# Gates' unit of the mLSTM: remainder and rounded weights in one stationary tile, and the norm's sums one unit later

## The chip, the cores and the metric

The kernel runs on one core of a Trainium2 chip. The metric is the device time of one execution in microseconds (us); 1,000 nanoseconds (ns) are 1 us.

## The reference, cut to what matters

The program is a transformer block followed by an mLSTM layer and an RG-LRU layer over 512 tokens of width 1024, all in fp32. The change lies at the start of the mLSTM layer:

```
u = rmsnorm(x, ln_g)
proj = u @ w_in                      # 1024 x (3*2048 + 8)
xm, z, o_pre, i_pre, f_pre = split(proj, [2048, 4096, 6144, 6148])
xc = silu(causal_dwconv(xm, conv_w, conv_b))
log_i = i_pre + b_i                  # 4 heads, 512 tokens
log_f = log_sigmoid(f_pre + b_f)
```

`i_pre` and `f_pre`, the gates, are 4 columns each: 8 columns of weights out of a tile that could hold 128.

## The kernel before, in words

Everything is kept transposed: features on the 128 partitions, the 512 tokens along the free dimension. A product of fp32 quality is made of three matmuls in a faster format (fp32r): each operand is split into a rounded part (`hi`) and the remainder (`lo`), and TensorE adds up `w_hi*u_hi`, `w_hi*u_lo` and `w_lo*u_hi` in one bank of PSUM. The helper `product` writes these three matmuls for each chunk k of 128 input features (L639, L640, L641); a unit of weights is 8 such blocks of 128 x 128, so a unit is 24 matmuls of 128 x 512.

The weights come as a stream of units through two slots. For each unit SyncE loads `w_raw`, ScalarE rounds it to `w_hi` (L1331, `hi(...)`, `split_raw`) as soon as the unit two places ahead of it in the stream has been used, VectorE subtracts to get `w_lo` (L2070, `lo(...)`, `split_lo`), and TensorE waits for that (`unit_ready`). The order of these steps among all other work of ScalarE and VectorE is written out by hand, and each engine works strictly in its order.

At the start of the mLSTM layer the order of units is G (gates), X(0,0), X(0,1), X(0,2), X(0,3), O(0,0), O(0,1), O(0,3), Q(0), .... The unit G has its 8 real columns in columns 0 to 3 (input gate) and 32 to 35 (forget gate) of each block; the other 120 columns are zeros. Before the stream of the layer can run freely, the last chunks of `u_hi` (ScalarE, L1357) and `u_lo` (VectorE, L2087) have to come, after the last additions to `x` (VectorE, L2101). TensorE therefore begins with chunks 0 to 6 of G, puts chunk 0 of X(0,0) before the wait for the last `u_lo`, takes chunk 7 of G, and goes on with X(0,0).

The scale of the norm is applied after the products. GpSimd adds up the squares (L3152), ScalarE rounds the sum (L1348, `sums_high(45)`), VectorE takes its remainder (L2074, `sums_low(3)`), and TensorE sums over partitions with matrices of ones (L1128 to L1130) into banks 3 and 4; this stands inside X(0,0), ahead of its chunk 6. Then ScalarE takes the root (L1762) and VectorE the reciprocal (L2643, `rstd`). In its hand-written order ScalarE does `sums_high(45)`, `hi(X(0,1))`, the root, `hi(X(0,2))`, `hi(X(0,3))`. VectorE does `sums_low(3)`, `lo(X(0,1))`, two small memsets (L2641), the reciprocal, the two reads of the gates' bank (L2647, L2648), `lo(X(0,2))`, the gates' biases (L2651, L2653), `f_abs` (L2654), the reading of X(0,0), `lo(X(0,3))`, and so on.

`linear_bank` gives the units three banks in turn, G included; `linear_free` waits until the bank's last reader is done.

Of the kernel before, what the change touches and what calls it, by code (L numbers as in the profile page):

```python
# [21 lines left out]
F32R = mybir.dt.float32r  # L22
# [4 lines left out]
P = 128  # L27
# [54 lines left out]
HELD_BANKS = (3, 4, 5, 6)  # L82
BRANCH_BANKS = (4, 6, 0, 2)
S_BANKS = (4, 5, 6, 3)
V_BANKS = (7, 4, 5, 6)
SW_AT = (0, 512, 896, 1152)
RX_BANKS = (0, 1, 3)
# [72 lines left out]
def unit_of(*name):  # L160
    return Lin(U_GATES + M_UNITS.index(name))
# [75 lines left out]
def build_program(nc, x_in, w_in, mat_in, vec_in, bias_in, rope_in, maskb_in, ident_in, causal_in, out):  # L237
    ctx = ExitStack()
    with ctx:
        def sb(name, shape, dt=F32, scope=ctx):  # L240
            return scope.enter_context(nc.sbuf_tensor(name, shape, dt))
# [17 lines left out]
        sums_hi, sums_lo = sums_r[:, 0, :], sums_r[:, 1, :]  # L259
        sumsq = sb("sumsq", [P, T])  # L260
        w_raw = sb("w_raw", [P, 2, UB * P])
        w_hi = sb("w_hi", [P, 2, UB * P], F32R)
        w_lo = sb("w_lo", [P, 2, UB * P], F32R)
        u_hi = sb("u_hi", [P, DC, T], F32R)
        u_lo = sb("u_lo", [P, DC, T], F32R)

# [365 lines left out]
        def _(pe):  # L632
# [13 lines left out]
            def unit_ready(n):  # L646
                pe.wait_ge(lo_ready, (n + 1).v())
# [317 lines left out]
            def linear_free(*name):  # L965

                i = M_LINEAR.index(name)
                if i < 2:
                    pe.wait_ge(bank_read, G_GATES - 2 + i + 3)
                elif i > 2:  # L970
                    before = M_LINEAR[i - 3]
                    if before[0] in "QK":
                        pe.wait_ge(qk_read, 4 * before[1] + 2 * "QK".index(before[0]) + before[2] + 1)
                    else:
                        pe.wait_ge(bank_read, evicted(*before))
# [131 lines left out]
            def linear_chunk(k, *name):  # L1107
                product(bank[linear_bank(*name)][:, :], [(k, u_hi[:, k, :], u_lo[:, k, :])], unit_of(*name), k == DC - 1,
                        start=k == 0, stop=k == DC - 1)

            unit_ready(unit_of("G"))
            linear_free("G")
            for k in range(DC - 1):
                pe.wait_ge(u_lo_ready, DC * 3 + k + 1)
                linear_chunk(k, "G")
            unit_ready(unit_of("X", 0, 0))
            linear_free("X", 0, 0)
            linear_chunk(0, "X", 0, 0)
            pe.wait_ge(u_lo_ready, DC * 3 + DC)
            linear_chunk(DC - 1, "G")  # L1120
            for k in range(1, DC):
                if k == 6:

                    pe.wait_ge(sq_added, 45)
                    pe.wait_ge(sums_lo_ready, 3)
                    for b in (3, 4):
                        if b == 3:
                            nc.tensor.matmul(bank[b][:, :], ones[:, :], sumsqb[:, :], start=True, stop=False)  # L1128
                        nc.tensor.matmul(bank[b][:, :], ones_r[:, :], sums_hi, start=b == 4, stop=False)
                        nc.tensor.matmul(bank[b][:, :], ones_r[:, :], sums_lo, start=False, stop=True).then_inc(stat_ready, 1)  # L1130
                linear_chunk(k, "X", 0, 0)
            for c in range(1, 4):
                linear("X", 0, c)
            for c in (0, 1, 3):
                linear("O", 0, c)
# [917 lines left out]
        def _(dve):  # L2053
# [589 lines left out]
            nc.vector.reciprocal(rstd[:, :], rms[:, :]).then_inc(rstd_ready, 1)  # L2643
            dve.wait_ge(rstd_ready, 4)
            unit_done(unit_of("G"))
            gb = bank[linear_bank("G")]
            step(nc.vector.tensor_tensor(i_row[:, :], gb[0:4, :], rstd[0:4, :], ALU.mult))  # L2647
            evict(nc.vector.tensor_tensor(f_row[:, :], gb[32:36, :], rstd[32:36, :], ALU.mult), "G")  # L2648
            lo("X", 0, 2)
            dve.wait_ge(bank_read, evicted("G"))  # L2650
            step(nc.vector.tensor_scalar(f_row[:, :], f_row[:, :], vecs[0:4, V_BIF + 1:V_BIF + 2], None, ALU.add))  # L2651
            step.wait()
            step(nc.vector.tensor_scalar(i_row[:, :], i_row[:, :], vecs[0:4, V_BIF:V_BIF + 1], None, ALU.add))  # L2653
            nc.vector.scalar_tensor_tensor(f_abs[:, :], f_row[:, :], -1.0, f_row[:, :], ALU.mult, ALU.max).then_inc(f_abs_ready, 1)  # L2654
            x_evict(0, 0)
            lo("X", 0, 3)
# [594 lines left out]
def weight_stream(a):  # L3251
    import numpy as np
    units = []

    def columns(w, c, rows=range(8)):
        units.append(blocks(w, [(r, c) for r in rows]))

    def ffn(gate_w, up_w, down_w):
        for c in range(F_PLAIN):
            columns(gate_w, c)  # L3260
            columns(up_w, c)
        for rows in DOWN_PARTS:
            for c in range(DC):
                columns(down_w, c, rows)


    order = np.concatenate([np.arange(HD * h, HD * (h + 1)) for j in range(4) for h in (j, j + 4)])
    ffn(a["ffn1_w_gate"][0], a["ffn1_w_up"][0], a["ffn1_w_down"][0])
    w = a["w_in"][0]
    for c in range(8):  # L3270
        columns(w, c)
    for part in range(4):
        units.append(wide(w[:, 1024:1536], 2 * part))
    qb = w[:, 1536:2048][:, order]
    for c in range(4):
        columns(qb, c)
    columns(w, 16)
    columns(w, 17)
    wb = a["w_branch_b"][0][order]
    for c in range(2 * DC):  # L3280
        columns(w, 18 + c)
    for c in range(DC):
        units.append(np.concatenate([blocks(a["w_branch_a"][0], [(r, c) for r in range(4)])[:, :4 * P],
                                     blocks(wb, [(r, c) for r in range(4)])[:, :4 * P]], axis=1))
    for c in range(DC):
        columns(a["w_out"][0], c)
    ffn(a["ffn2_w_gate"][0], a["ffn2_w_up"][0], a["ffn2_w_down"][0])

    w = a["m_w_in_2"][0]
    gates = np.zeros((D, P), np.float32)  # L3290
    gates[:, 0:4] = w[:, 6144:6148]
    gates[:, 32:36] = w[:, 6148:6152]
    for name in M_UNITS:
        kind = name[0]
        if kind == "G":
            columns(gates, 0)
        elif kind in "XZO":
            columns(w, 16 * "XZO".index(kind) + 4 * name[1] + name[2])
        elif kind in "QK":
            units.append(blocks(a["m_w_q_2" if kind == "Q" else "m_w_k_2"][0, name[1]], [(r, e) for e in range(2) for r in range(4)]))  # L3300
        elif kind == "V":
            units.append(wide(a["m_w_v_2"][0, name[1]], 2 * name[2]))
        else:
            h, k = name[1:]
            units.append(blocks(a["m_w_out_2"][0], [(4 * h + r, 2 * k + e) for e in range(2) for r in range(4)]))
    w = a["r_w_in_2"][0]
    for p in range(4):
        for base in (0, 12):
            for c in range(3):
                columns(w, base + 3 * p + c)  # L3310
        for wg in (a["r_w_a_2"][0], a["r_w_x_2"][0]):
            pair = np.zeros((3 * P, 3 * P), np.float32)
            pair[0:192, 0:192] = wg[2 * p]
            pair[192:384, 192:384] = wg[2 * p + 1]
            units.append(blocks(pair, GATE_BLOCKS))
    for part in range(2):
        for c in range(DC):
            columns(a["r_w_out_2"][0], c, range(6 * part, 6 * part + 6))
    while len(units) < U_ALL:
        units.append(np.zeros((P, UB * P), np.float32))  # L3320
    assert len(units) == U_ALL
    return np.stack(units)
# [93 lines left out]
```

## Time and profile before

| | |
|---|---|
| time, median of 3 runs | 1779.04 us (1778.79 to 1779.22) |
| time of the profiled execution | 1780.06 us |
| its span (first to last instruction) | 1778.2 us |
| TensorE matmul busy | 1766.3 us, 99% |
| VectorE busy | 1223.2 us, 69% |
| ScalarE busy | 850.6 us, 48% |
| GpSimd busy | 266.0 us, 15% |
| TensorE's clock, mean over the span | 0.997 of full speed |

In the profile PE is TensorE's matmuls, PEld its weight loads (they overlap the matmuls), DVE is VectorE, ACT ScalarE, POOL GpSimd and SP SyncE. The end of a matmul is modelled, and matmuls overlap, so the start of one to the start of the next is the time that it costs.

### The profile page before, as it was taken

How to read it: one execution, taken by the hardware profiler on the slowest of the kernel's cores; microseconds unless marked ns; L12 is line 12 of the kernel's file. 1: busy time of each engine (PE TensorE's matmuls, PEld its weight loads, DVE VectorE, ACT ScalarE, POOL GpSimd, SP SyncE). 2: the span in 40 equal slices, each digit the busy share in tenths (PEclk: the TensorE clock that was granted, in tenths of full speed). 3: DMA queues.
4: the chain of work that ended last, by engine and by line, in shares of the span. 5: the costliest groups of instructions: out<-in, count | busy, mean ns of one | idle time of the engine just before them, and what ended most of it. 6: DMA issues, size and time to landing. Idle time of an engine off the chain costs nothing.

```text
span 1778.2 us, 24809 instructions
## 1 busy us (share of the span) xinstructions
PE 1766.3 (99%) x9474; PEld 1506.6 (85%) x9474; DVE 1223.2 (69%) x1473; ACT 850.6 (48%) x1197; POOL 266.0 (15%) x270
## 2 busy tenths in 40 slices
PE   9999999999999999999999999999999999999997
PEld 7899989888777788889989888888888888888886
DVE  6778657543777655678747567887586677868984
ACT  5445335424555544345425465453353444466663
POOL 3011010211000002001101330200101101213333
PEclk9999999999999999999999999999999999999998
DMA  6345342344221225345434223232222222223243
GB/s 239 109 133 174 121 132 71 105 148 142 87 70 59 83 95 174 98 121 176 143 105 121 72 96 112 79 99 85 95 83 89 95 83 83 94 96 106 96 131 107
DMA packets 56151, 195.94 MB, mean 110 GB/s; under 512 B 6680, under 2 KB 8856, under 8 KB 56048
## 3 DMA queue, kind: packets, MB, share of 16 engines
q1 hardware_dynamic: 39408, 135.55, 23.2%
q0 software_dynamic: 16208, 58.55, 11.0%
q8 instruction: 73, 1.20, 0.3%
q10 hardware_dynamic: 432, 0.40, 0.1%
q14 instruction: 30, 0.25, 0.0%
HBM read 190.26 MB, written 2.11 MB: 108 GB/s over the span
## 4 chain that ended last, share of the span: by engine, by line
PE 99%; DMA 0%; DVE 0%; ACT 0%; POOL 0%; POOLq 0%; issue 0%; ACTq 0%; DVEq 0%
PE banks L639 24%; PE banks L641 23%; PE banks L640 23%; PE banks L758 6%; PE banks L757 6%; PE banks L756 6%; PE banks L855 1%; PE banks L874 1%; PE banks L898 1%; PE banks L1033 1%; PE banks L1035 1%; PE banks L1034 1%; PE banks L1061 0%; PE banks L1059 0%; PE banks L1060 0%; PE banks L818 0%
## 5 line engine op out<-in xcount | busy, mean ns | idle before, releaser
L2070 DVE TENSOR_TENSOR w_lo<-w_raw,w_hi 128x1024 fp32r<-128x1024 f32 x249 | 316.9, 1273 | 305.3 <-ACT w_hi L1331 304.2
L1331 ACT ACTIVATE w_hi<-w_raw 128x1024 fp32r<-128x1024 f32 x249 | 263.3, 1058 | 379.2 <-PE banks L641 337.6
L639 PE MATMUL banks<-u_hi,w_hi 128*128 128x512 f32 x1016 | 400.6, 394 | 0.6 <-DVE u_lo L2087 0.6
L641 PE MATMUL banks<-u_hi,w_lo 128*128 128x512 f32 x1016 | 395.8, 390 | 0.0
L640 PE MATMUL banks<-u_lo,w_hi 128*128 128x512 f32 x1016 | 395.4, 389 | 0.0
L639 PEld LDWEIGHTS banks<-u_hi,w_hi 128*128 128x128 f32 x1016 | 190.8, 188 | 42.2 <-issue 2.2
L641 PEld LDWEIGHTS banks<-u_hi,w_lo 128*128 128x128 f32 x1016 | 190.7, 188 | 40.7
L640 PEld LDWEIGHTS banks<-u_lo,w_hi 128*128 128x128 f32 x1016 | 190.9, 188 | 38.7 <-issue 0.5
L758 PE MATMUL banks<-xs_hi,w_lo 128*128 128x256 f32 x512 | 144.9, 283 | 0.0
L757 PE MATMUL banks<-xs_lo,w_hi 128*128 128x256 f32 x512 | 144.9, 283 | 0.0
L756 PE MATMUL banks<-xs_hi,w_hi 128*128 128x256 f32 x512 | 144.9, 283 | 0.0
L639 PE MATMUL banks<-hid_hi,w_hi 128*128 128x512 f32 x352 | 137.3, 390 | 0.0
L640 PE MATMUL banks<-hid_lo,w_hi 128*128 128x512 f32 x352 | 137.0, 389 | 0.0
L641 PE MATMUL banks<-hid_hi,w_lo 128*128 128x512 f32 x352 | 137.0, 389 | 0.0
L3080 POOL TENSOR_TENSOR sumsq<-sumsq,sq 128x512 f32<-128x512 f32 x38 | 57.8, 1521 | 343.9 <-ACT sq L1340 342.9
L756 PE MATMUL banks<-u_hi,w_hi 128*128 128x256 f32 x384 | 108.7, 283 | 0.0
L757 PE MATMUL banks<-u_lo,w_hi 128*128 128x256 f32 x384 | 108.7, 283 | 0.0
L758 PE MATMUL banks<-u_hi,w_lo 128*128 128x256 f32 x384 | 108.7, 283 | 0.0
L756 PEld LDWEIGHTS banks<-xs_hi,w_hi 128*128 128x128 f32 x512 | 98.3, 192 | 0.2
L757 PEld LDWEIGHTS banks<-xs_lo,w_hi 128*128 128x128 f32 x512 | 98.3, 192 | 0.2
L758 PEld LDWEIGHTS banks<-xs_hi,w_lo 128*128 128x128 f32 x512 | 98.3, 192 | 0.0
L1443 ACT ACTIVATE w_hi<-m 128x1024 fp32r<-128x1024 f32 x64 | 67.2, 1054 | 62.0 <-DVE m L2217 39.3
(390 smaller groups left out, 3434.9 us busy)
## 6 DMA issues: line engine op xcount, KB each, us to landing
w_raw<-weights SPq DMA_DIRECT2D x251, 512.0 KB, 3.5
m<-matrices POOLq DMA_DIRECT2D x48, 512.0 KB, 4.5
mx<-matrices POOLq DMA_DIRECT2D x32, 512.0 KB, 5.0
m_even<-matrices POOLq DMA_DIRECT2D x8, 512.0 KB, 7.0
sq<-matrices POOLq DMA_DIRECT2D x8, 512.0 KB, 6.9
bias<-neighbour_bias POOLq DMA_DIRECT2D x8, 384.0 KB, 5.1
v_win<-v_a POOLq DMA_DIRECT2D x16, 128.0 KB, 4.7
out_t<-x SPq DMA_DIRECT2D x16, 128.0 KB, 1.8
```

The lines of the kernel that those rows point to most:

```text
L639: nc.tensor.matmul(o, wh, hi, start=start and k == 0, stop=False)
L640: nc.tensor.matmul(o, wh, lo, start=False, stop=False)
L641: ins = nc.tensor.matmul(o, wl, hi, start=False, stop=stop and k == len(pairs) - 1)
L756: nc.tensor.matmul(half_bank, wh[:, b], hi, start=fresh and c == 0 and kk == 0, stop=False, skip_group_check=True)
L757: nc.tensor.matmul(half_bank, wh[:, b], lo, start=False, stop=False, skip_group_check=True)
L758: ins = nc.tensor.matmul(half_bank, wl[:, b], hi, start=False, stop=kk == 3, skip_group_check=True)
L855: ins = nc.tensor.matmul(bank[4 + 2 * (t % 2) + e][:, 0:nk], q_t, k_t, start=True, stop=True)
L874: ins = nc.tensor.matmul(o, v_t, prob_t[:, s % 2, e, b * P:(b + 1) * P], start=b == 0, stop=b == nb - 1)
L1331: nc.scalar.activation(w_hi[:, n.slot, :], w_raw[:, n.slot, :], ACT.Copy).then_inc(hi_ready, 1)
L1443: nc.scalar.activation(slot_of(w_hi, w_hi2, j), product_source(k, p), ACT.Copy).then_inc(m_hi, 1)
L2070: nc.vector.tensor_tensor(w_lo[:, n.slot, :], w_raw[:, n.slot, :], w_hi[:, n.slot, :].bitcast(F32), ALU.subtract)\
L3080: nc.gpsimd.tensor_tensor(sumsq[:, :], sumsq[:, :], sq[:, m % 2, :], ALU.add).then_inc(sq_added, 1)
```

## The change

The unit G's split is now one strided tile. The host lays out G's weights so that a column's 8 chunks lie next to each other (16 places apart, 8 of them used), and `w_hi` and `w_lo` become the two halves of one tile `w_split`. A slice of it with a stride of 16 elements (64 bytes) is a stationary matrix with the rounded gates in its columns 0 to 63 and the remainders in columns 64 to 127. One matmul with `u_hi` and one with `u_lo` give, in 128 partitions of one bank, the products of both parts: 16 matmuls for 24. VectorE then has to add partitions 64 to 67 to 0 to 3, and 96 to 99 to 32 to 35. G gets bank 7 for itself. TensorE puts three chunks of X(0,0) before the wait for the last `u_lo`, and the norm's sums move from X(0,0), ahead of chunk 6, to X(0,1), ahead of chunk 1.

```diff
@@ build_program
-        w_hi = sb("w_hi", [P, 2, UB * P], F32R)
-        w_lo = sb("w_lo", [P, 2, UB * P], F32R)
+        w_split = sb("w_split", [P, 2, 2, UB * P], F32R)
+        w_hi, w_lo = w_split[:, :, 0, :], w_split[:, :, 1, :]
@@ TensorE, linear_free
-                    if before[0] in "QK":
+                    if before[0] == "G":
+                        pe.wait_ge(bank_read, G_GATES - 2 + 3)
+                    elif before[0] in "QK":
@@ TensorE, start of the layer
+            def gates_chunk(k):
+                both = w_split[:, unit_of("G").slot, :, :].rearrange("p a b -> p (a b)")[:, k::2 * UB]
+                nc.tensor.matmul(bank[GATES_BANK][:, :], both, u_hi[:, k, :], start=k == 0, stop=False)
+                ins = nc.tensor.matmul(bank[GATES_BANK][:, :], both, u_lo[:, k, :], start=False, stop=k == DC - 1)
+                if k == DC - 1:
+                    ins.then_inc(unit_used, 1)
             unit_ready(unit_of("G"))
-            linear_free("G")
             for k in range(DC - 1):
                 pe.wait_ge(u_lo_ready, DC * 3 + k + 1)
-                linear_chunk(k, "G")
+                gates_chunk(k)
             unit_ready(unit_of("X", 0, 0))
             linear_free("X", 0, 0)
-            linear_chunk(0, "X", 0, 0)
+            for k in range(3):
+                linear_chunk(k, "X", 0, 0)
             pe.wait_ge(u_lo_ready, DC * 3 + DC)
-            linear_chunk(DC - 1, "G")
-            for k in range(1, DC):
-                if k == 6:
+            gates_chunk(DC - 1)
+            for k in range(3, DC):
+                linear_chunk(k, "X", 0, 0)
+            unit_ready(unit_of("X", 0, 1))
+            linear_free("X", 0, 1)
+            for k in range(DC):
+                if k == 1:
                     pe.wait_ge(sq_added, 45)
                     pe.wait_ge(sums_lo_ready, 3)
...
-                linear_chunk(k, "X", 0, 0)
-            for c in range(1, 4):
+                linear_chunk(k, "X", 0, 1)
+            for c in range(2, 4):
                 linear("X", 0, c)
@@ VectorE, after the reciprocal
-            gb = bank[linear_bank("G")]
+            gb = bank[GATES_BANK]
+            i_low, f_low = m_row, e_row
+            step(nc.vector.tensor_tensor(i_low[:, :], gb[64:68, :], rstd[64:68, :], ALU.mult))
+            step(nc.vector.tensor_tensor(f_low[:, :], gb[96:100, :], rstd[96:100, :], ALU.mult))
             step(nc.vector.tensor_tensor(i_row[:, :], gb[0:4, :], rstd[0:4, :], ALU.mult))
             evict(nc.vector.tensor_tensor(f_row[:, :], gb[32:36, :], rstd[32:36, :], ALU.mult), "G")
             lo("X", 0, 2)
             dve.wait_ge(bank_read, evicted("G"))
-            step(nc.vector.tensor_scalar(f_row[:, :], f_row[:, :], vecs[0:4, V_BIF + 1:V_BIF + 2], None, ALU.add))
             step.wait()
-            step(nc.vector.tensor_scalar(i_row[:, :], i_row[:, :], vecs[0:4, V_BIF:V_BIF + 1], None, ALU.add))
+            step(nc.vector.scalar_tensor_tensor(f_row[:, :], f_row[:, :], vecs[0:4, V_BIF + 1:V_BIF + 2], f_low[:, :],
+                                                ALU.add, ALU.add))
+            step.wait()
+            step(nc.vector.scalar_tensor_tensor(i_row[:, :], i_row[:, :], vecs[0:4, V_BIF:V_BIF + 1], i_low[:, :],
+                                                ALU.add, ALU.add))
@@ host, weight_stream
         if kind == "G":
-            columns(gates, 0)
+            unit = np.zeros((P, UB * P // 16, 16), np.float32)
+            unit[:, :, :DC] = gates[:, :UB * P // 16].reshape(DC, P, UB * P // 16).transpose(1, 2, 0)
+            units.append(unit.reshape(P, UB * P))
```

## Rows read from the trace of the kernel before

**Rows 1.** the page: span, busy time, and the chain that ended last

```profile
span 1778.2 us, 24809 instructions
...
PE 1766.3 (99%) x9474; PEld 1506.6 (85%) x9474; DVE 1223.2 (69%) x1473; ACT 850.6 (48%) x1197; POOL 266.0 (15%) x270
...
PE 99%; DMA 0%; DVE 0%; ACT 0%; POOL 0%; POOLq 0%; issue 0%; ACTq 0%; DVEq 0%
```

**Rows 2.** timeline of TensorE's matmuls (start us, duration us, line) around the change

```profile
1034.61 0.39 PE L639 MATMUL banks<-u_hi,w_hi 128*128 128x512 f32 x1
...
1039.82 0.39 PE L641 MATMUL banks<-u_hi,w_lo 128*128 128x512 f32 x1
1040.05 0.43 PE L639 MATMUL banks<-u_hi,w_hi 128*128 128x512 f32 x1
...
1044.21 1.02 PE L1128 MATMUL banks<-sumsqb,ones_r 128*128 128x512 f32 x2
...
1045.30 0.39 PE L1130 MATMUL banks<-sums_r,ones_r 128*128 128x512 f32 x1
...
1045.99 0.40 PE L639 MATMUL banks<-u_hi,w_hi 128*128 128x512 f32 x1
```

**Rows 3.** timeline of VectorE there (in brackets: idle before, and its releaser)

```profile
1036.16 1.23 DVE L2070 TENSOR_TENSOR w_lo<-w_raw,w_hi 128x1024 fp32r<-128x1024 f32 x1 [1.20 <-ACT w_hi L1331]
...
1039.17 0.75 DVE L2087 SCALAR_TENSOR_TENSOR u_lo<-x,gg,u_hi  x1 [1.19 <-ACT u_hi L1357]
1043.20 0.69 DVE L2074 TENSOR_TENSOR sums_r<-sumsq,sums_r 128x512 fp32r<-128x512 f32 x1 [3.28 <-ACT sums_r L1348]
1044.15 1.23 DVE L2070 TENSOR_TENSOR w_lo<-w_raw,w_hi 128x1024 fp32r<-128x1024 f32 x1 [0.26 <-ACT w_hi L1331]
...
1046.45 3.35 DVE L2643 RECIPROCAL rstd<-rms 128x512 f32<-128x512 f32 x1 [1.05 <-ACT rms L1762]
1049.84 0.68 DVE L2647 TENSOR_TENSOR g_row<-banks,rstd 4x512 f32<-4x512 f32 x1
...
1051.26 1.23 DVE L2070 TENSOR_TENSOR w_lo<-w_raw,w_hi 128x1024 fp32r<-128x1024 f32 x1
1052.40 0.47 DVE L2651 TENSOR_SCALAR g_row<-g_row,vecs 4x512 f32<-4x512 f32 x1
...
1054.62 1.22 DVE L2070 TENSOR_TENSOR w_lo<-w_raw,w_hi 128x1024 fp32r<-128x1024 f32 x1
```

**Rows 4.** timeline of ScalarE, same stretch

```profile
1042.54 0.63 ACT L1348 ACTIVATE sums_r<-sumsq 128x512 fp32r<-128x512 f32 x1 [2.39 <-POOL sumsqb L3152]
1043.08 1.04 ACT L1331 ACTIVATE w_hi<-w_raw 128x1024 fp32r<-128x1024 f32 x1
...
1045.73 0.69 ACT L1762 ACTIVATE rms<-banks,eps 128x512 f32<-128x512 f32 x1 [0.30 <-PE banks L1130]
```

**Rows 5.** timeline of weight loads (PEld) and matmuls among products of 256 columns

```profile
850.25 0.19 PEld L757 LDWEIGHTS banks<-xs_lo,w_hi 128*128 128x128 f32 x1
...
850.25 0.28 PE L756 MATMUL banks<-xs_hi,w_hi 128*128 128x256 f32 x1
850.37 0.28 PE L757 MATMUL banks<-xs_lo,w_hi 128*128 128x256 f32 x1
```

**Rows 6.** windows: us, busy (instructions) of PE, PEld, DVE, ACT, POOL, PEclk granted

```profile
1765.10:1767.40 2.30, 1.12 (x10) 0.95 (x9) 2.20 (x7) 0.68 (x2) 0.00 (x0) 1.00 0.67 231
1767.40:1767.60 0.20, 0.20 (x2) 0.20 (x3) 0.15 (x1) 0.00 (x0) 0.00 (x0) 0.80 0.94 338
1767.60:1768.00 0.40, 0.40 (x4) 0.40 (x3) 0.00 (x0) 0.00 (x0) 0.00 (x0) 0.50 0.69 236
```

**Rows 7.** the line of the start's matmuls of ones: duration ns min/median/max

```profile
L671 PE MATMUL banks<-ones_r x8: 592/1061/1222, 1.1 to 6.7; 128*128 128x512 f32 x8
```

**Rows 8.** timeline of VectorE before unit Q(0)

```profile
1077.45 1.21 DVE L2070 TENSOR_TENSOR w_lo<-w_raw,w_hi 128x1024 fp32r<-128x1024 f32 x1
...
1080.21 0.69 DVE L2526 TENSOR_TENSOR o_sig<-banks,rstd 128x512 f32<-128x512 f32 x1 [0.95 <-PE banks L641]
```

More of the change, by code:

```diff
@@ L84 @@
 S_BANKS = (4, 5, 6, 3)
+GATES_BANK = 7
 V_BANKS = (7, 4, 5, 6)
```

## The prediction, made before the change was run

> **What bounds the kernel.** I read the page first: TensorE's matmuls cover 1766.3 of 1778.2 us and the chain that ended last is 99% TensorE [rows 1]. So a matmul that goes saves its pitch, and a wait of TensorE that appears is paid in full, because there is no later idle time that could take it back. Next I read the timelines of the four engines around the start of the mLSTM layer and asked of each unit of weights when it is ready and when TensorE comes to it. TensorE runs through without a pause: 24 matmuls from 1034.61 to 1040.05 give a pitch of 5.44 / 24 = 0.2267 us, and the norm's five sums take 1045.99 - 1044.21 = 1.78 us [rows 2]. VectorE and ScalarE have small idle gaps, but their hand-written order gives moments that TensorE cannot hurry: the remainder of X(0,0) is ready at 1037.39, the last `u_lo` at 1039.92, the remainder of X(0,1) at 1044.15 + 1.23 = 1045.38, that of X(0,2) at 1051.26 + 1.23 = 1052.49 [rows 3]. From the order in the source, the write at 1044.15 is X(0,1)'s: it is the one between `sums_low(3)` (L2074) and the reciprocal (L2643). ScalarE rounds X(0,1) only after `sums_high(45)`, which waits for GpSimd's last addition [rows 4]. None of this depends on how many matmuls G has.
>
> TensorE before comes to X(0,1) at 1045.99 + 6 x 0.2267 = 1047.35, 1.97 us after it is ready, and to X(0,2) at 1045.99 + 30 x 0.2267 = 1052.79, only 0.30 us after it is ready. That second margin is what the change touches most.
>
> **The change, part by part**
>
> *Eight matmuls less.* 8 x 0.2267 = 1.81 us of TensorE, if nothing waits.
>
> *The wait for the last `u_lo`.* After the change 14 + 9 = 23 matmuls stand before it and TensorE arrives at 1034.61 + 23 x 0.2267 = 1039.82. The value comes at 1039.92, and before the change the matmul behind it started at 1040.05 [rows 2, 3]. It will start there again: 0.23 us of the 1.81 is lost. X(0,0) is needed at 1034.61 + 14 x 0.2267 = 1037.78, 0.39 after it is ready: no wait.
>
> *X(0,1) becomes urgent.* 17 matmuls remain (2 of G, 15 of X(0,0)): TensorE is through at 1040.05 + 17 x 0.2267 = 1043.90. Before, the norm's sums stood here and filled the time; now they stand behind chunk 0 of X(0,1), whose remainder ends at 1045.38. A restart takes some 0.17 us from the end of the producer (1039.92 to 1040.05 and the longer first matmul, 0.43 for 0.39 [rows 2, 3]), so TensorE goes on at 1045.55: a wait of 1.65 us, most of the saving. From here on the time is set by ScalarE and VectorE, not by G.
>
> *The norm's sums come later.* They start at 1045.55 + 3 x 0.2267 = 1046.23, 2.02 us later than 1044.21. The root, the reciprocal and all behind them on VectorE follow by the same 2.02, as the root waited for the sums and the reciprocal for the root [rows 3, 4].
>
> *Two reads more in VectorE's queue.* The gates' bank is now read four times. The nearest rows are the reads of the other two row groups, at a pitch of (1051.26 - 1049.84) / 2 = 0.71 us [rows 3]: 1.42 us. They stand ahead of `lo(X(0,2))`. So X(0,2) is ready at 1052.49 + 2.02 + 1.42 = 1055.93, and TensorE starts it at 1056.10. TensorE has only 21 matmuls of X(0,1) left behind the sums, where there were 30: it is through at 1046.23 + 1.78 + 21 x 0.2267 = 1052.77 and stands still for 3.3 us. Before it began X(0,2) at 1052.79; it is now 1056.10 - 1052.79 = 3.3 us late.
>
> *Behind that.* The two bias steps become three-operand additions, at most 0.68 for 0.47 [rows 3]: 0.4 us on VectorE. `lo(X(0,3))` then starts at 1054.62 + 3.44 + 0.4 = 1058.5 and is ready at 1059.7; TensorE needs it at 1056.10 + 5.44 = 1061.5. VectorE stays 3.9 us late and TensorE 3.3, so the tightest later margin is unit Q(0): ready at 1078.66, needed at 1045.99 + 150 x 0.2267 = 1080.0 [rows 2, 8], 1.3 us, which shrinks to some 0.8. Then comes a wait of VectorE for TensorE of 0.95 us [rows 8], and the two are in step again. No third wait. The bank of G, the other banks (each read 3 us and more ahead), the changed `linear_free` and GpSimd's mask load behind the sums cost nothing: bank 7 is idle here, and the rest is shifted with TensorE.
>
> *The strided weight load.* No row shows a stationary operand with a 64-byte step. Below it costs nothing: in products of 256 columns matmuls follow each other every 0.12 us though each has its own load of 128 columns [rows 5], so at a pitch of 0.2267 a load may take about 0.107 us longer and stay hidden. Above I let the load take one matmul's pitch more, 0.2 us in each of the 16. The waits for `u_lo` and X(0,1) cover 1045.55 - (1034.61 + 40 x 0.2267) = 1.87 us, or 0.117 per load; the upper bound would leave 16 x 0.2 - 1.87 = 1.3 us on the path. I take nothing. The Trainium skill ("SBUF — State Buffer", in "Door 1: The DMA port swizzle", on SBUF cachelines) says that accesses which each go to another 16-byte line pay a penalty, which speaks against this load; it gives no figure. If it halved the rate, a load would take at most 0.24 us for the 0.12 of [rows 5], which the pitch and the cover still hide, so the sum stays.
>
> *TensorE's clock.* The granted clock is 1.00 right through the start of the layer, but TensorE never stands still for long there. At the end of the program the last dense matmuls end at 1765.1, only a few small ones follow, and the clock is down to 0.50 (1.2 GHz) from about 1767.5: 2.4 us later [rows 6]. The new wait is 3.3 us long. So I expect that the clock falls in it or just behind it. Price: at the start the matmuls of ones take 1061 ns, and 592 at full clock; the first starts at 1.1, the last, at full clock, by 6.7 [rows 7], so at most 5.6 us of matmuls at half speed, which is 2.8 us lost; below, nothing. Both rows are taken at the ends of the program, with pauses between matmuls; behind this wait the matmuls are dense, so I take a little over the middle, 1.6 us. The Trainium skill ("TensorE: Matmul & The Clock Gate", "Part 1: The HAM clock gate") has the same two levels and says that activity releases the throttle; [rows 6] agrees as to the fall.
>
> **Sum.** -1.81 + 0.23 + 1.65 + 3.33 = +3.3 (rounding 0.1, the same as 1056.10 - 1052.79), and with the clock +1.6 = +4.9 us. Against the profiled execution: 1780.06 + 4.9 = 1785.0. The median of the runs lies 1.02 below the profiled one, so 1779.04 + 4.9 = 1783.9.
>
> A measurement of this kernel can tell about 0.2%, here 3.6 us, from no change. The forecast without the clock (3.3) lies just inside.
>
> **The rivals**
>
> *A, both waits and the clock falls: 1783.9.* For it the row at the end [rows 6]; against it that this row has small matmuls, not dense ones with a gap.
>
> *B, both waits, the clock stays: 1782.3.* For it that the clock is 1.00 in all of the middle; against it that no pause there is as long.
>
> *C, the strided load is slow too: up to 1.3 more on B or A, 1783.6 to 1785.2.* It decides from 0.117 us per load on.
>
> *D, faster: the X(0,1) remainder is not the write at 1044.15 but the one before it.* If I have the stream off by one unit, the write at 1044.15 is X(0,2)'s, and the one at 1051.26 X(0,3)'s. Then neither wait exists, and -1.81 + 0.23 = -1.6 is kept: 1777.5. Against it: between 1036.16 and 1044.15 VectorE writes no remainder at all [rows 3], and the source has `lo(X(0,1))` right behind `sums_low(3)`. It decides if X(0,2) is ready before 1051.2.
>
> *E, the strided loads slow nothing and the waits are short: about 1780 to 1781.* It would need a reciprocal or a root that is not in the chain; [rows 3, 4] speak against it.
>
> **How the numbers follow.** Chances: A 0.58, B 0.27, C 0.07, D 0.04, E 0.04. The predicted time is A's, 1783.9. Range: down to B less 0.5 for E's nearer part, 1781.8; up to the upper bound of the clock, 1779.04 + 3.3 + 2.8 = 1785.1, and a part of C: 1785.7. Slower by over 0.2% (from 1782.6) are A, C and a tenth of B: 0.67. Within 0.2% is the rest of B, E and a little: 0.29. Faster by over 0.2% would need more than 3.6 us, over D's 1.6: D falls within 0.2% too, and 0.01 is left; so 0.67, 0.32, 0.01.
>
> **What the profile after would show.** TensorE idle for about 1.65 us ahead of X(0,1), released by L2070, and for about 3.3 us ahead of X(0,2), released by L2070; the reciprocal about 2.0 us later, four reads of the gates at 0.71; a granted clock under 1.00 in one stretch at the second wait and matmuls at a pitch of about 0.43 there; weight loads of G near 0.19 to 0.3 us with a pitch of 0.227. Wrong would be: no wait ahead of X(0,2) (step "two reads more" or the order), a clock of 1.00 all through (A), or a pitch in G above 0.34 (the load).

## The result, and the profile after

| | before | after |
|---|---|---|
| median | 1778.93 us | 1783.91 us |
| lowest and highest of 8 runs | 1778.79 to 1779.52 | 1782.89 to 1784.98 |
| span of the profiled execution | 1778.2 | 1781.8 |
| TensorE matmul instructions | 9474 | 9466 |

The ratio is 1.0029, with a 95% interval of 1.0018 to 1.0039: slower by 4.98 us. The predicted 1783.9 was met to 0.01 us. The runs after spread three times as wide as those before.

The page of the changed kernel, to be held against [rows 1]:

```profile
span 1781.8 us, 24796 instructions
...
PE 1765.2 (99%) x9466; PEld 1506.4 (85%) x9466; DVE 1225.1 (69%) x1475; ACT 850.3 (48%) x1197; POOL 266.0 (15%) x270
...
PE 98%; DVE 1%; issue 0%; ACT 0%; DMA 0%; POOL 0%; ACTq 0%; DVEq 0%; POOLq 0%
```

TensorE does 8 matmuls less and is busy 1.1 us less, but VectorE has come into the chain that ended last, with 1%. The timeline of TensorE's matmuls, against [rows 2] (start and duration in us; in brackets the idle time before and what ended it):

```profile
1033.90 0.40 PE L1117 MATMUL banks<-u_hi,w_split 128*128 128x512 f32 x1
1034.13 0.40 PE L1118 MATMUL banks<-u_lo,w_split 128*128 128x512 f32 x1
...
1037.41 0.47 PE L640 MATMUL banks<-u_hi,w_split 128*128 128x512 f32 x1
...
1039.55 0.40 PE L1117 MATMUL banks<-u_hi,w_split 128*128 128x512 f32 x1
...
1044.72 0.50 PE L640 MATMUL banks<-u_hi,w_split 128*128 128x512 f32 x1 [1.10 <-DVE w_split L2085]
...
1045.52 1.02 PE L1143 MATMUL banks<-sumsqb,ones_r 128*128 128x512 f32 x2
...
1047.31 0.40 PE L640 MATMUL banks<-u_hi,w_split 128*128 128x512 f32 x1
...
1055.28 0.50 PE L640 MATMUL banks<-u_hi,w_split 128*128 128x512 f32 x1 [3.01 <-DVE w_split L2085]
...
1056.13 0.63 PE L640 MATMUL banks<-u_hi,w_split 128*128 128x512 f32 x1
1056.56 0.63 PE L641 MATMUL banks<-u_lo,w_split 128*128 128x512 f32 x1
...
1059.12 0.54 PE L641 MATMUL banks<-u_lo,w_split 128*128 128x512 f32 x1
...
1059.72 0.40 PE L640 MATMUL banks<-u_hi,w_split 128*128 128x512 f32 x1
```

In this execution the layer starts 0.71 us earlier (1033.90 for 1034.61), so all that follows is read as time since G's first matmul. The norm's sums (L1143) start at 11.62 after 9.60 before, 2.02 us later. X(0,2) starts at 1055.28, that is 21.38; before it was at 18.18 (1052.79 by the prediction's counting). With the longer first matmul after a pause (0.34 to the next one for 0.23) that is 3.3 us late. And from 1056.13 to 1059.12 matmuls follow each other every 0.427 us: half speed.

VectorE, against [rows 3]:

```profile
1035.44 1.23 DVE L2085 TENSOR_TENSOR w_split<-w_raw,w_split 128x1024 fp32r<-128x1024 f32 x1 [1.20 <-ACT w_split L1346]
1036.59 0.68 DVE L2116 SCALAR_TENSOR_TENSOR x<-banks,x 128x512 f32 x1
1038.46 0.75 DVE L2102 SCALAR_TENSOR_TENSOR u_lo<-x,gg,u_hi  x1 [1.19 <-ACT u_hi L1372]
...
1043.44 1.23 DVE L2085 TENSOR_TENSOR w_split<-w_raw,w_split 128x1024 fp32r<-128x1024 f32 x1 [0.26 <-ACT w_split L1346]
...
1047.75 3.35 DVE L2658 RECIPROCAL rstd<-rms 128x512 f32<-128x512 f32 x1 [3.07 <-ACT rms L1777]
1051.14 0.69 DVE L2663 TENSOR_TENSOR g_row<-banks,rstd 4x512 f32<-4x512 f32 x1
...
1054.00 1.22 DVE L2085 TENSOR_TENSOR w_split<-w_raw,w_split 128x1024 fp32r<-128x1024 f32 x1
1055.15 0.73 DVE L2670 SCALAR_TENSOR_TENSOR g_row<-g_row,vecs 4x512 f32<-4x512 f32 x1
...
1057.89 1.22 DVE L2085 TENSOR_TENSOR w_split<-w_raw,w_split 128x1024 fp32r<-128x1024 f32 x1
```

The remainder of X(0,1) is written at 1043.44, which is 9.54 after G's first matmul, as before. The reciprocal begins 2.01 us later than before (13.85 for 11.84), four reads of the gates' bank follow at a pitch of 0.715, and the remainder of X(0,2) ends at 1054.00 + 1.22 = 1055.22, 0.06 before TensorE's first load of X(0,2). The windows over the second wait show the clock (us, busy time and instructions of PE, PEld, DVE, ACT, POOL, then PEclk, the granted clock):

```profile
1052.40:1055.20 2.80, 0.00 (x0) 0.00 (x0) 2.71 (x5) 2.31 (x2) 0.00 (x0) 1.00 0.00 0
1056.00:1059.00 3.00, 3.00 (x9) 2.33 (x8) 2.97 (x4) 1.69 (x2) 0.00 (x0) 0.50 0.57 175
1060.00:1062.00 2.00, 2.00 (x10) 1.65 (x9) 1.93 (x4) 0.38 (x1) 0.00 (x0) 1.00 0.77 256
```

TensorE does nothing at all from 1052.4 to 1055.2; the clock is still 1.00 there, it is 0.50 (1.2 GHz) just behind, and 1.00 again at 1060. The 11 matmuls from 1055.28 to 1059.49 take 4.21 us, where at full clock they would take 0.34 and ten times 0.23: eight of them lost 0.2 us each, 1.6 us.

The weight loads (start, duration):

```profile
1034.13 0.30 PEld L1117 LDWEIGHTS banks<-u_hi,w_split 128*128 128x128 f32 x1
...
1037.38 0.19 PEld L640 LDWEIGHTS banks<-u_hi,w_split 128*128 128x128 f32 x1 [0.35 <-issue]
...
1044.72 0.19 PEld L640 LDWEIGHTS banks<-u_hi,w_split 128*128 128x128 f32 x1 [1.52 <-DVE w_split L2085]
...
1055.28 0.19 PEld L640 LDWEIGHTS banks<-u_hi,w_split 128*128 128x128 f32 x1 [3.43 <-DVE w_split L2085]
```

A load of G with its 64-byte step takes 0.30 us for 0.19. It is hidden but for 0.009: the pitch in G is (1036.96 - 1033.90) / 13 = 0.235 for 0.227.

The gates' transposition behind unit K(0) starts at 1095.23, which is 61.33 us after G's first matmul; before it was 1091.00 and 56.39. So the changed kernel is 4.94 us late there, and it stays so until the last stage: GpSimd's last addition of squares, 1767.85 after and 1763.55 before, is 5.0 us late by the same count.

The profiled span is only 3.6 longer. Of the difference 0.71 is the earlier start of the layer, 0.65 of it already there at 26 us into the program; its cause is open. Another 0.7 is the end of the program, which this change does not touch. There the same eight small matmuls took, first before and then after,

```profile
1767.28 1.88 PE L1299 MATMUL banks<-ident,rstd_last 128*128 128x128 f32 x8 [0.55 <-DVE rstd_last L3037]
1771.58 1.16 PE L1314 MATMUL banks<-ident,rstd_last 128*128 128x128 f32 x8 [0.55 <-DVE rstd_last L3058]
```

and their granted clock is 0.50 before [rows 6] and 1.00 after:

```profile
1771.70:1772.00 0.30, 0.30 (x3) 0.30 (x4) 0.14 (x1) 0.00 (x0) 0.00 (x0) 1.00 0.96 338
```

In the 13 profiles of this case these eight matmuls are slow in three (before, e2, e6: 1.75 to 1.98 us) and take 1.16 us in ten. So a time of the whole program holds up to 0.8 us that comes and goes with the clock at its end, whatever the change.

### The profile page after: what moved, and what is told of

It reads as the page before. It is cut to its first block, busy times and chain, and to the rows that moved or that the text cites. A ratio compares the mean times of both kernels' runs of the same rounds, so it can differ in the third digit from the quotient of the medians.

```text
span 1781.8 us, 24796 instructions
## 1 busy us (share of the span) xinstructions
PE 1765.2 (99%) x9466; PEld 1506.4 (85%) x9466; DVE 1225.1 (69%) x1475; ACT 850.3 (48%) x1197; POOL 266.0 (15%) x270
## 4 chain that ended last, share of the span: by engine, by line
PE 98%; DVE 1%; issue 0%; ACT 0%; DMA 0%; POOL 0%; ACTq 0%; DVEq 0%; POOLq 0%
PE banks L640 23%; PE banks L642 23%; PE banks L641 23%; PE banks L758 6%; PE banks L759 6%; PE banks L757 6%; PE banks L856 1%; PE banks L875 1%; PE banks L899 1%; PE banks L1038 1%; PE banks L1036 1%; PE banks L1037 1%; PE banks L1064 0%; PE banks L1062 0%; PE banks L1063 0%; PE banks L819 0%
## 5 line engine op out<-in xcount | busy, mean ns | idle before, releaser
L2085 DVE TENSOR_TENSOR w_split<-w_raw,w_split 128x1024 fp32r<-128x1024 f32 x249 | 317.0, 1273 | 305.9 <-ACT w_split L1346 304.9
L1346 ACT ACTIVATE w_split<-w_raw 128x1024 fp32r<-128x1024 f32 x249 | 263.3, 1058 | 379.5 <-PE banks L642 338.3
L640 PE MATMUL banks<-u_hi,w_split 128*128 128x512 f32 x1008 | 398.4, 395 | 5.3 <-DVE w_split L2085 4.1
L642 PE MATMUL banks<-u_hi,w_split 128*128 128x512 f32 x1008 | 393.4, 390 | 0.0
L641 PE MATMUL banks<-u_lo,w_split 128*128 128x512 f32 x1008 | 393.1, 390 | 0.0
L640 PEld LDWEIGHTS banks<-u_hi,w_split 128*128 128x128 f32 x1008 | 189.6, 188 | 47.0 <-DVE w_split L2085 5.8
L642 PEld LDWEIGHTS banks<-u_hi,w_split 128*128 128x128 f32 x1008 | 189.7, 188 | 40.3
L641 PEld LDWEIGHTS banks<-u_lo,w_split 128*128 128x128 f32 x1008 | 189.9, 188 | 38.6 <-issue 0.5
L640 PE MATMUL banks<-hid_hi,w_split 128*128 128x512 f32 x352 | 137.3, 390 | 0.0
L641 PE MATMUL banks<-hid_lo,w_split 128*128 128x512 f32 x352 | 137.1, 389 | 0.0
L642 PE MATMUL banks<-hid_hi,w_split 128*128 128x512 f32 x352 | 137.0, 389 | 0.0
L640 PEld LDWEIGHTS banks<-hid_hi,w_split 128*128 128x128 f32 x352 | 66.1, 188 | 14.6 <-DVE hid_lo L2089 1.0
L642 PEld LDWEIGHTS banks<-hid_hi,w_split 128*128 128x128 f32 x352 | 66.1, 188 | 13.7
L759 PE MATMUL banks<-xs_hi,w_split 128*128 128x256 f32 x256 | 72.5, 283 | 0.0
L757 PE MATMUL banks<-xs_hi,w_split 128*128 128x256 f32 x256 | 72.5, 283 | 0.0
```

The source lines that it names most:

```text
L640: nc.tensor.matmul(o, wh, hi, start=start and k == 0, stop=False)
L641: nc.tensor.matmul(o, wh, lo, start=False, stop=False)
L642: ins = nc.tensor.matmul(o, wl, hi, start=False, stop=stop and k == len(pairs) - 1)
L757: nc.tensor.matmul(half_bank, wh[:, b], hi, start=fresh and c == 0 and kk == 0, stop=False, skip_group_check=True)
L759: ins = nc.tensor.matmul(half_bank, wl[:, b], hi, start=False, stop=kk == 3, skip_group_check=True)
L1346: nc.scalar.activation(w_hi[:, n.slot, :], w_raw[:, n.slot, :], ACT.Copy).then_inc(hi_ready, 1)
```

## The experiments

Each time stands beside that of the kernel before on the same chips. The differences are 0.01 to 0.3%, and some of the intervals hold 1; so what a reading rests on is the place and the length of the waits in the profile, beside which the medians stand. The last column is from the profiles: the time from G's first matmul to the gates' transposition, less the 56.39 us of the kernel before. It leaves out both ends of the program.

| run | median us | before us | difference | ratio, 95% interval | stretch in the profile |
|---|---|---|---|---|---|
| changed kernel | 1783.91 | 1778.93 | +4.98 | 1.0018 to 1.0039 | +4.94 |
| e1, sums back in X(0,0) | 1780.22 | 1779.31 | +0.91 | 0.9997 to 1.0015 | +1.21 |
| e2, remainder of X(0,2) first | 1781.46 | 1779.31 | +2.15 | 1.0004 to 1.0022 | +2.20 |
| e3, new order alone | 1780.99 | 1779.31 | +1.68 | 1.0001 to 1.0019 | +1.88 |
| e4, filler in the second wait | 1782.46 | 1779.31 | +3.15 | 1.0008 to 1.0026 | +3.37 |
| e5, contiguous loads | 1784.56 | 1779.38 | +5.18 | 1.0017 to 1.0040 | +6.08 |
| e6, two reads, not four | 1781.37 | 1779.38 | +1.99 | 1.0002 to 1.0020 | +1.89 |
| e7, sums between, remainder first | 1779.24 | 1779.38 | -0.14 | 0.9990 to 1.0008 | +0.13 |
| e8, reordered further | 1779.10 | 1779.38 | -0.28 | 0.9989 to 1.0007 | -0.07 |
| e10, Q's remainders earlier too | 1778.04 | 1779.01 | -0.97 | 0.9987 to 1.0005 | -0.96 |

**e1: the norm's sums back inside X(0,0).**

```diff
@@ from the changed kernel, TensorE
             for k in range(3, DC):
+                if k == 6:
+                    ...
                 linear_chunk(k, "X", 0, 0)
-            unit_ready(unit_of("X", 0, 1))
-            linear_free("X", 0, 1)
-            for k in range(DC):
-                if k == 1:
-                    ...
-                linear_chunk(k, "X", 0, 1)
-            for c in range(2, 4):
+            for c in range(1, 4):
                 linear("X", 0, c)
```

> The changed kernel with the norm's sums back in X(0,0), ahead of chunk 6. Theory of the waits (the time is set by when the remainders of X(0,1) and X(0,2) come): TensorE waits about 1.4 us for the remainder of the sums, then nothing ahead of X(0,1), then about 1.3 us ahead of X(0,2), because the two more reads of the gates' bank (1.42 us) still stand before it; clock 1.00 through; 1780.0 us, 1.1 over the kernel before. Rival, the strided loads cost: 1783.9, unchanged. Rival, the later sums alone cost: 1777.3.

TensorE's two waits in it:

```profile
1043.57 1.10 PE L1139 MATMUL banks<-sumsqb,ones_r 128*128 128x512 f32 x2 [1.05 <-DVE sums_r L2085]
...
1053.42 0.50 PE L640 MATMUL banks<-u_hi,w_split 128*128 128x512 f32 x1 [1.01 <-DVE w_split L2081]
```

The first is for the remainder of the sums, the second, 1.0 us long, is X(0,2)'s. The clock stayed up. The time is +0.91 (+1.21 in the profile's stretch) for the expected 1.1; the strided loads are all still there and cost nothing to be seen.

**e2: the remainder of X(0,2) ahead of the four reads.**

```diff
@@ from the changed kernel, VectorE
+            lo("X", 0, 2)
             unit_done(unit_of("G"))
             gb = bank[GATES_BANK]
...
-            lo("X", 0, 2)
             dve.wait_ge(bank_read, evicted("G"))
```

> The changed kernel with the remainder of X(0,2) ahead of the four reads of the gates' bank in VectorE's order. Theory of the waits: 1.5 us ahead of X(0,1) stays, the wait ahead of X(0,2) shrinks from 3.0 to about 0.5 us, but VectorE is full here, so about 1.2 us turn up ahead of X(0,3) and about 0.5 ahead of Q(0); clock 1.00 through; 1780.6 to 1781.2. Rival, the strided loads cost: 1783.9. Rival, the two waits are all there is: 1779.4.

Measured 1781.46 (+2.15), 0.3 above the upper end of what was expected. The weight loads that had to wait for a remainder, ahead of X(0,1), X(0,2) and X(0,3):

```profile
1044.93 0.19 PEld L640 LDWEIGHTS banks<-u_hi,w_split 128*128 128x128 f32 x1 [1.51 <-DVE w_split L2085]
...
1052.63 0.19 PEld L640 LDWEIGHTS banks<-u_hi,w_split 128*128 128x128 f32 x1 [0.56 <-DVE w_split L2085]
...
1059.50 0.19 PEld L640 LDWEIGHTS banks<-u_hi,w_split 128*128 128x128 f32 x1 [1.55 <-DVE w_split L2085]
```

The wait ahead of X(0,2) is down from 3.4 to 0.56 us of the loads' row, and 1.55 us have turned up one unit later, where 1.2 were expected; ahead of Q(0) hardly anything came (0.36 us from one matmul to the next for 0.23) where 0.5 were expected. Moving work about on VectorE moves the wait along: from the reciprocal to Q(0) that engine has hardly any free time (in this run it is busy for 29.3 of the 30.25 us from 1047.75 to 1078).

**e3: TensorE's new order alone, from the kernel before.**

```diff
@@ from the kernel before, TensorE
-            linear_chunk(0, "X", 0, 0)
+            for k in range(3):
+                linear_chunk(k, "X", 0, 0)
             pe.wait_ge(u_lo_ready, DC * 3 + DC)
             linear_chunk(DC - 1, "G")
-            for k in range(1, DC):
-                if k == 6:
-                    ...
+            for k in range(3, DC):
                 linear_chunk(k, "X", 0, 0)
-            for c in range(1, 4):
+            unit_ready(unit_of("X", 0, 1))
+            linear_free("X", 0, 1)
+            for k in range(DC):
+                if k == 1:
+                    ...
+                linear_chunk(k, "X", 0, 1)
+            for c in range(2, 4):
```

> The kernel before (24 matmuls of G, two reads, separate w_hi and w_lo) with TensorE's new order alone: three chunks of X(0,0) before the last u_lo, the norm's sums in X(0,1) ahead of chunk 1. Theory of the waits: hardly a wait ahead of X(0,1), 1.9 us ahead of X(0,2), clock 1.00; 1780.8. The difference to the changed kernel is then the two reads (1.4) and the fallen clock (1.6). Rival, the strided tile costs: 1778.9, as before.

+1.68, with one long wait, 1.57 us, ahead of X(0,2) (and 0.21 us of the loads' row ahead of X(0,1)):

```profile
1054.13 0.50 PE L639 MATMUL banks<-u_hi,w_hi 128*128 128x512 f32 x1 [1.57 <-DVE w_lo L2075]
```

**e6: the changed kernel with two reads of the gates.** It leaves out the product of the gates with the weights' remainder.

```diff
@@ from the changed kernel, VectorE
-            step(nc.vector.tensor_tensor(i_low[:, :], gb[64:68, :], rstd[64:68, :], ALU.mult))
-            step(nc.vector.tensor_tensor(f_low[:, :], gb[96:100, :], rstd[96:100, :], ALU.mult))
...
-            step(nc.vector.scalar_tensor_tensor(f_row[:, :], f_row[:, :], vecs[0:4, V_BIF + 1:V_BIF + 2], f_low[:, :],
-                                                ALU.add, ALU.add))
+            step(nc.vector.tensor_scalar(f_row[:, :], f_row[:, :], vecs[0:4, V_BIF + 1:V_BIF + 2], None, ALU.add))
```

> The changed kernel without the two reads of the remainders' rows and without their additions: the gates lack the product with the remainder of the weights. Theory of the waits: the wait ahead of X(0,2) shrinks by 1.4 to about 1.6 to 1.9 us, the clock stays at 1.00, and the time is that of the new order alone, 1780.8: the 8 matmuls that went are worth nothing. Rival, they are worth their pitch: 1779.0. Rival, the clock falls in a wait of this length too: 1782.4.

1781.37 (+1.99) for the expected 1780.8, and the same second wait as e3's:

```profile
1054.57 0.50 PE L640 MATMUL banks<-u_hi,w_split 128*128 128x512 f32 x1 [1.57 <-DVE w_split L2085]
```

e3 and e6 differ by the eight matmuls (and the strided tile). e6 has them not, and is no faster: from G's first matmul to the transposition it takes 58.28 us, e3 58.27. In this order they are worth nothing. In these waits of 1.57 us the clock stayed at 1.00.

**e4: filler.** 13 matmuls more, into a bank that is overwritten.

```diff
@@ from the changed kernel, TensorE
                 linear_chunk(k, "X", 0, 1)
+            linear_free("X", 0, 2)
+            for k in range(13):
+                nc.tensor.matmul(bank[linear_bank("X", 0, 2)][:, :], ones_r[:, :], u_hi[:, k % DC, :], start=True, stop=True)
             for c in range(2, 4):
                 linear("X", 0, c)
```

> The changed kernel with 13 matmuls of 128 x 512 more, in the wait ahead of X(0,2), into the bank that X(0,2) then overwrites. Theory of the clock: X(0,2) starts as late as in the changed kernel, but the clock stays at 1.00, so 1782.2, 1.7 less than the changed kernel, and with less spread over the runs. Rival, the clock is not worth anything or falls all the same: 1783.9. Rival, more matmuls cost their pitch: 1786.9.

Its windows over the second wait and behind it:

```profile
1052.00:1055.00 3.00, 3.00 (x15) 2.47 (x14) 2.88 (x5) 2.34 (x2) 0.00 (x0) 1.00 0.00 0
1056.00:1059.00 3.00, 3.00 (x15) 2.43 (x14) 2.93 (x5) 1.45 (x2) 0.00 (x0) 1.00 0.53 175
```

X(0,2) begins as late as in the changed kernel, 21.39 us after G's first matmul (at 1034.13) for 21.38:

```profile
1055.52 0.19 PEld L640 LDWEIGHTS banks<-u_hi,w_split 128*128 128x128 f32 x1 [0.45 <-DVE w_split L2088]
```

The clock stays at 1.00 and +4.98 becomes +3.15, while TensorE does 13 matmuls more. The runs lie within 0.8 us (1782.26 to 1783.09) and no longer within 2.1. So 3.15 (3.37 in the profile's stretch) is the price of the waits, the 3.3 of the sum. The clock's price is 1.57 us in the profile's stretch, just what the eight slow matmuls lost. By the medians it is 1.45 (1783.91 less 1782.46), or 1.8 as the difference of the two differences, since the two medians of the kernel before are 0.4 apart.

**e5: contiguous loads.** The gates are computed from other weights.

```diff
-                both = w_split[:, unit_of("G").slot, :, :].rearrange("p a b -> p (a b)")[:, k::2 * UB]
+                both = w_split[:, unit_of("G").slot, :, :].rearrange("p a b -> p (a b)")[:, k * P:(k + 1) * P]
```

> The changed kernel with G's 16 stationary operands read as 128 consecutive columns in place of every 16th: the gates are then computed from other weights, the instructions are the same. Theory of the waits: the loads of G get back to 0.19 us from 0.30, the pitch in G to 0.227 from 0.235, and the time stays at 1783.9 (up to 0.5 by the clock), because TensorE waits behind G anyway. Rival, the strided loads cost: 1780.6 or less.

The loads are back at 0.19 us and at a pitch of 0.23,

```profile
1034.16 0.19 PEld L1118 LDWEIGHTS banks<-u_lo,w_split 128*128 128x128 f32 x1
1034.39 0.19 PEld L1117 LDWEIGHTS banks<-u_hi,w_split 128*128 128x128 f32 x1
```

and the time is 1784.56 (+5.18), no faster than the changed kernel; 1783.9 to 1784.4 were expected. X(0,0) begins 3.52 us after G's first matmul for 3.51 with the strided loads, and here the record names what it waits for:

```profile
1037.68 0.47 PE L640 MATMUL banks<-u_hi,w_split 128*128 128x512 f32 x1 [0.19 <-DVE x L2116]
```

In its profiled execution the clock is down already within the wait, which TensorE's last matmul (start 1052.17) opens and the one at 1055.57 ends. It stays down over 14 matmuls, for eight in the changed kernel's, and 2.7 us are lost for 1.6:

```profile
1052.60:1054.40 1.80, 0.00 (x0) 0.00 (x0) 1.71 (x4) 1.72 (x2) 0.00 (x0) 1.00 0.00 0
1054.60:1055.50 0.90, 0.00 (x0) 0.00 (x0) 0.90 (x2) 0.42 (x1) 0.00 (x0) 0.50 0.00 0
1056.00:1059.00 3.00, 3.00 (x8) 2.32 (x8) 2.93 (x5) 1.41 (x2) 0.00 (x0) 0.50 0.55 175
1059.00:1062.00 3.00, 3.00 (x9) 2.31 (x9) 2.89 (x5) 1.66 (x3) 0.00 (x0) 0.60 0.47 150
1063.00:1065.00 2.00, 2.00 (x10) 1.65 (x9) 0.00 (x0) 0.86 (x1) 0.00 (x0) 1.00 0.00 0
```

That one took 1785.08, 0.5 above its median. How long the clock stays down thus differed between the two executions that have a profile. That the runs of the changed kernel spread for this reason is likely, as the spread is gone in e4, but no second profile of that kernel shows it.

**e7, e8, e10: can the saving be kept?** e7 puts the sums between X(0,0) and X(0,1), where the remainder of the sums is just ready, and has e2's edit:

```diff
@@ e7, from e2, TensorE
             for k in range(3, DC):
                 linear_chunk(k, "X", 0, 0)
-            unit_ready(unit_of("X", 0, 1))
-            linear_free("X", 0, 1)
-            for k in range(DC):
-                if k == 1:
-                    ...
-                linear_chunk(k, "X", 0, 1)
-            for c in range(2, 4):
+            pe.wait_ge(sq_added, 45)
+            pe.wait_ge(sums_lo_ready, 3)
+            ...
+            for c in range(1, 4):
```

> The changed kernel with the norm's sums between X(0,0) and X(0,1), and the remainder of X(0,2) ahead of the reads of the gates' bank. Theory of the waits, with VectorE full from the reciprocal to Q(0): no wait ahead of X(0,1) and X(0,2), 1.2 us ahead of X(0,3), 0.7 to 1.0 ahead of Q(0); 1779.2 to 1779.4, so the saving of 1.6 is given back on VectorE. Rival, the two waits were all that stood against the saving: 1777.4.

The time is the expected one, -0.14, and the only long wait is ahead of X(0,3); ahead of Q(0) there is 0.17 us in place of the 0.7 to 1.0:

```profile
1057.66 0.50 PE L640 MATMUL banks<-u_hi,w_split 128*128 128x512 f32 x1 [0.93 <-DVE w_split L2079]
```

e8 moves more of VectorE's and ScalarE's work:

```diff
@@ e8, from e7
             evict(nc.vector.tensor_tensor(f_row[:, :], gb[32:36, :], rstd[32:36, :], ALU.mult), "G")
+            x_evict(0, 0)
+            lo("X", 0, 3)
...
-            x_evict(0, 0)
-            lo("X", 0, 3)
             x_conv(0, 0)
...
-            for c in range(3):
-                xc_lo_part(0, c)
+            xc_lo_part(0, 0)
             o_evict(0, 0)
-            o_evict(0, 1)
             lo("Q", 0)
+            xc_lo_part(0, 1)
+            xc_lo_part(0, 2)
+            o_evict(0, 1)
             xc_lo_part(0, 3)
@@ ScalarE
             hi("X", 0, 3)
+            hi("O", 0, 0)
             act.wait_ge(f_abs_ready, 1)
...
-            hi("O", 0, 0)
```

> As the run before, and also: reading of X(0,0) and the remainder of X(0,3) ahead of the gates' biases, ScalarE's rounding of O(0,0) ahead of its exponential, the remainder of Q(0) ahead of two remainders of xc and the second reading of O. Theory: the first unit that comes late is O(0,0), by 0.4 us; 1777.8, 1.1 under the kernel before. Rival, VectorE's 1.8 us more come back somewhere: 1778.9 or more.

-0.28; expected were -1.1. What I had missed stands behind Q(0), where TensorE now waits for the bank that `q_lo` reads:

```profile
1086.60 0.39 PE L642 MATMUL banks<-xch,w_split 128*128 128x512 f32 x1
1087.61 0.50 PE L640 MATMUL banks<-xch,w_split 128*128 128x512 f32 x1 [0.62 <-DVE q_lo L2577]
```

From one matmul to the next it is 1.01 us there for 0.23. VectorE comes to `q_lo` only after the scans of the gates. e10 puts it ahead of the second scan:

```diff
@@ e10, from e8, VectorE
+            q_or_k_lo("Q", 0)
             step(nc.vector.tensor_tensor_scan(m_row[:, :], f_abs[:, :], a_row[:, :], 0.0, ALU.mult, ALU.max))
             step.wait()
             nc.vector.tensor_scalar(neg_m[:, :], m_row[:, :], -1.0, None, ALU.mult).then_inc(gates_dve, 1)
-            q_or_k_lo("Q", 0)
```

> The reordered kernel with VectorE's two remainders of Q(0), which free the banks of unit O(0,2) and the one before it, ahead of the second scan of the gates (in the reordered kernel TensorE waits 0.8 us there for q_lo). Theory: TensorE keeps all but the 0.3 us that it waits at O(0,0) and O(0,1): 1.2 us under the kernel before, 0.9 under the reordered kernel. Rival, the wait turns up again behind: no less than 0.3 under the kernel before.

-0.97 for the expected -1.2: 1777.78 to 1779.33 in 11 runs, against 1778.71 to 1779.82 in 15 of the kernel before. That is the fastest of these kernels by its median and by its lowest run, but at 0.05% it is inside the interval of the ratio. The profile's stretch is shorter by the same 0.96 us, in one execution of each. It is as near as I came to a version that beats both.

**e9 and e11: what a strided load costs by itself.** In the products of 256 columns, where a pitch of 0.12 us gives a load no cover [rows 5], the stationary columns are taken with a step. The products are computed from other weights.

```diff
@@ e9, from the kernel before, pair_product
-                        b = slice((2 * kk + c) * P, (2 * kk + c + 1) * P)
+                        b = slice(2 * kk + c, None, 8) if f == 0 else slice(2 * kk + c, 2 * kk + c + 2 * P, 2)
@@ e11
+                        b = slice(2 * kk + c, 2 * kk + c + 4 * P, 4) if f == 0 else slice(2 * kk + c, 2 * kk + c + 3 * P, 3)
```

> The kernel before, with other stationary operands in the products of 256 columns: in the first FFN every 8th column (a step of 32 bytes), in the second every 2nd (8 bytes); 1344 matmuls each; the products are computed from other weights. Theory, a load whose columns each lie in another 16 bytes takes about 0.11 us longer (0.30 for 0.19 in the changed kernel's G): pitch in the first FFN's products 0.12 to about 0.23 us, in the second's unchanged 0.12; 1780 + 148 = 1928 us. Rival, a step of 32 bytes is free and only 64 bytes cost: 1780. Rival, every step other than 1 costs: 2076.

> As the run with steps of 32 and 8 bytes, now 16 bytes in the first FFN's products of 256 columns and 12 bytes in the second's; computed from other weights. Theory, what counts is whether the next column lies in another 16 bytes: pitch 0.24 us at 16 bytes, and between 0.18 and 0.24 at 12. Rival, the cost grows with the step: 0.18 at 16 bytes, 0.15 at 12.

e9 in the first FFN, a load and two matmuls:

```profile
210.12 0.34 PEld L758 LDWEIGHTS banks<-xs_hi,w_lo 128*128 128x128 f32 x1
```

```profile
210.26 0.40 PE L758 MATMUL banks<-xs_hi,w_lo 128*128 128x256 f32 x1
210.50 0.41 PE L756 MATMUL banks<-xs_hi,w_hi 128*128 128x256 f32 x1
```

| step | pitch of the 256-column matmuls |
|---|---|
| 4 bytes | 0.120 us |
| 8 bytes | 0.120 |
| 12 bytes | 0.176 |
| 16 bytes | 0.233 |
| 32 bytes | 0.240 |

The times, of one execution each, agree: 1941.43 us is 161.6 over the 1779.84 beside it (148 was expected, from 0.11 per load), and 1344 matmuls at 0.12 more are 161. e11 took 2006.72, 227.7 over 1779.01; 1344 x (0.113 + 0.056) is 227. The Trainium skill ("SBUF — State Buffer", "Door 1: The DMA port swizzle") says that accesses which each go to another 16-byte line pay a penalty, and that at least two hits on a line are needed to absorb it. These rows agree: two columns to a line are free, one to a line doubles the pitch, and steps of 12 bytes, three in four of which reach a new line, lie between. An estimate from the table: if a new line costs as much as two columns, the 96 lines of 128 columns at 12 bytes cost 192 / 128 = 1.5 times 0.120, which is 0.18 for the 0.176 measured.

## Why the prediction was right

- *Eight matmuls less, 1.81 us.* The count is right, the saving is not to be seen, as forecast: e3 and e6.
- *The wait for the last `u_lo`, 0.23 us.* Here a wait came that I had ruled out. TensorE's first load of X(0,0) is at 1037.38, 0.35 us idle, though its remainder was ready at 1036.67. It follows the addition to `x` (1036.59 + 0.68 = 1037.27), the last reader of the bank that X(0,0) takes; e5's record names it. `linear_free` was near, not "3 us and more ahead": in the kernel before, this addition ended at 1037.98 and TensorE came at 1039.37, 1.4 us later. The step cost 0.3 us, about what `u_lo` would have, and then the `u_lo` wait was gone. Both are covered by the wait behind. That the two balance is luck.
- *The wait ahead of X(0,1), 1.65 us.* TensorE would have gone on at 1043.46 and does at 1044.72: 1.26, and 1.37 with the longer first matmul, as the 1.65 counts it (the loads' row shows 1.52). It is 0.3 shorter because TensorE came 0.27 later, with the slower G and the wait above. The sum does not move, since the end of the wait is where it was forecast: the remainder is ready 10.77 us after G's first matmul.
- *Sums 2.02 us later; four reads at 0.71.* 2.02 and 0.715.
- *The wait ahead of X(0,2), 3.33 us, and 3.3 in all.* By the same count 3.27 us (3.43 in the loads' row); X(0,2) 3.3 late; e4 gives 3.15 for the sum without the clock. The four terms add up to 3.40, not 3.3; what the prediction calls rounding is that the kernel before was itself 0.08 slower than its pitch of 0.2267 between 1040.05 and 1044.21.
- *The biases, 0.4 us on VectorE.* 0.73 and 0.74 for 0.47 twice, 0.53, and over the 0.68 that I had as the most; why, no run shows. No third wait came.
- *The strided load, 0 taken.* It is 0.11 us slower, at my limit of 0.107, so 0.009 a matmul shows; rival C is out (e5).
- *The clock, 1.6 us.* It fell, and 1.6 was lost in the profiled run; over the runs it is 1.45 to 1.8. The size is a lucky hit: it was a choice a little over the middle of 0 to 2.8, and e5's profile lost 2.7. The row that it rested on, the clock's fall at the end of the program [rows 6], is not one to rest on either: at the same place the clock stayed up in ten of the 13 profiles, the changed kernel's own among them. The fall behind the wait of about 3 us came in both profiles that have such a wait empty.

Rivals B, D and E are out: the granted clock of 0.50 and e4 against B, the two waits in the profile against D and E.

## What to carry to other kernels

An engine at 99% of the span does not yet mean that less work on it is less time: ask for each piece of input when it is ready, and by how much. Here two margins, 1.97 and 0.30 us, were smaller than what a moved block of 1.78 us and two small reads took from them. A block of work whose input is late (the norm's sums) is filler for what stands behind it: put it where its own input has just come, not later. And when TensorE would wait for about 3 us, as here, count the clock's fall too, or give it something to do. Last, before a row of the profile carries a term of a few tenths of a microsecond, look whether other executions show it too.

## What the runs showed of the hardware

A stationary load of 128 fp32 columns takes 0.12 us of the pitch, and up to 0.24 with one column to every 16 bytes. A matmul of 512 columns (0.227) hides all but 0.009 of the extra time, one of 256 (0.120) hides none of it. The granted clock stayed at 1.00 in waits of 1.0 to 1.6 us. It fell with one of 3.0 to 3.4 us, for eight matmuls in one profile and 14 in another. In the first the fall came when TensorE had begun again (the first two matmuls ran at full speed), in the other already within the wait; either way the time lost is behind the wait. The Trainium skill ("TensorE: Matmul & The Clock Gate", "HAM oscillation — how this bites in real kernels") describes a kernel in which a long wait for data lets the clock fall, so that the next matmuls start slow. These two profiles agree, but for the two matmuls that still ran fast in the first. At the end of the program, behind a stretch of some 2.3 us in which TensorE is busy for about half of the time, the clock fell in three profiles (one is [rows 6]) and stayed at 1.00 in the ten others.
